# Weighted sums of the prompt attention in two bursts of 32 matmuls instead of one of 64

## The chip, the cores and the metric

The kernel runs on one core of one Trainium2 chip. The metric is the device time of one execution in microseconds (us). In the profile PE is TensorE's matmul row, PEld its weight loads, DVE is VectorE, ACT is ScalarE, POOL is GpSimd and SP is SyncE, whose queue (SPq) issues most DMAs. TensorE's clock has two levels here, 2.4 GHz (granted clock 1.0) and 1.2 GHz (0.5).

## What is computed

One step of a one-layer decoder trunk: an input projection to nine groups of columns, four token mixers side by side, an output projection, and a squared-ReLU MLP. There are 2048 prompt tokens and 8 x 4 sample tokens. What the change touches is the third mixer on the prompt, a strictly causal stick-breaking attention with four heads of 64 channels; its last line is the weighted sum of the values:

```python
def sb_block(q, k, v, q_start, sb_bias):
    z = jnp.einsum('bqhd,bkhd->bhqk', q, k) * (HEAD_DIM ** -0.5) + sb_bias[None, :, None, None]
    mask = kpos[None, :] < qpos[:, None]
    l = jnp.where(mask, jax.nn.log_sigmoid(-z), 0.0)
    later = jnp.flip(jnp.cumsum(jnp.flip(l, -1), -1), -1) - l
    w = jnp.where(mask, jnp.exp(jax.nn.log_sigmoid(z) + later), 0.0)
    return jnp.einsum('bhqk,bkhd->bqhd', w, v)
```

## The kernel before

**Dense work.** The projections and the MLP run over five blocks of 416 tokens. After the input projection the program is a list of steps. One step is one [128 x 1024] weight tile against one block: for each of eight groups of 128 channels it issues three matmuls of 128 x 416 (high part of the weights times high and low part of the activations, low part of the weights times the high part), 24 in all, into one of three PSUM banks. `dense(n)` writes one step; its loop over `groups` is the list of the eight. ACT and DVE split each weight tile into its two parts two steps ahead, read the finished bank, and prepare the next activations.

**Attention.** It is cut into 40 sets of (512 queries, a head, 512 keys), and each set into four units of 128 queries. The units are laid over time slots `tau`. The first 20 slots lie in the last steps of the input projection (two slots in a step). Those from 20 on lie one in a dense step, by the table `SLOT_AT`, in the first three of the MLP's stretches; this is the second part of the attention. In a slot TensorE computes the scores of one unit (lines 931 and 932), ACT takes two sigmoids of them, DVE makes the running product (`scan`), the product of both and its transpose in blocks of 32, in the following slots.

**Weighted sums.** `weigh(v)` takes all four units of set v at once: the keys are cut into 16 blocks of 32, and for every block there are four quarters of 32 rows, so that the array works as eight tiles of 32 x 64. The loop over `k` takes two blocks at a time, with 2 x 4 matmuls (line 946), in all 64. The trace shows each of them as two, so 128 matmuls and 128 weight loads. In the diagonal sets (queries and keys of one chunk) only the columns behind the diagonal are computed, 128, 96, 64 and 32 of them. The sums of all sets of a head and chunk pile up in PSUM banks 3 to 6. In front of the loop TensorE waits for the values (`s_vin3`), for the four transposes (`s_wt`) and, for the first set of a head, for the banks (`s_yc`); behind it, it signals `s_av`.

**Who waits for that signal.** After the last set of a head ACT copies half of the sums (`low_part`, line 1379) and DVE adds them; SP loads the next set's values (`load_v`, line 697); DVE's transposes of the set after next use the buffer anew. `weigh` is called in every fourth slot by `attention(tau)`, which stands ahead of `dense(n)` in the list of steps: scores, then weighted sum, then 24 matmuls of the step.

The order on each engine is the order in which the program writes it; nothing rearranges it. Instructions of TensorE come by DMA, on the queue that the profile calls q8.

Of the kernel before, what the change touches and what calls it, by code (L numbers as in the profile page):

```python
# [52 lines left out]
CHW = 512  # L53
# [56 lines left out]
def base_of(b):  # L110

    return PRE + STEPS_B * b
# [40 lines left out]
N_SETS, N_UNITS = len(SETS), 4 * len(SETS)  # L153
FIRST = [SETS.index((c, h, c)) for c in range(CH) for h in range(NH)]
FINAL = [SETS.index((c, h, 0)) for c in range(CH) for h in range(NH)]
ALONE = 20
SLOTS = N_UNITS + 4
SHARE = (46, 52, SLOTS - ALONE - 98)
SLOT_AT = {}
# [85 lines left out]
def build(nc, x_all, w_all, pvec, lnp, rows2, gates_a, gates_x, poolw, sbh, sbr, masks, ident_d, ck, cv, ptab,  # L245
          st_h, st_a, st_b, st_p, y_out, kv_out, so_out):
    ctx = ExitStack()
    with ctx:
# [10 lines left out]
        def sem(name):  # L259
            return ctx.enter_context(nc.semaphore(name))  # L260
# [63 lines left out]
        def x_hi(b):  # L324

            return xearly[:, b, 0, :, :] if b < 2 else xlate[:, b - 2, 0, :, :]

        def x_lo(b):

            return xearly[:, b, 1, :, :] if b < 2 else xlate[:, b - 2, 1, :, :]  # L330
# [146 lines left out]
        s_wt, s_av = sem("w_turned"), sem("av_done")  # L477
# [364 lines left out]
        def _(pe):  # L842
# [77 lines left out]
            def scores(t):  # L920

                v, i, w, top = unit(t)
                if i == 0:
                    pe.wait_ge(s_klo, v + 1)
                    if v in FIRST:
                        pe.wait_ge(s_qlo, FIRST.index(v) + 1)
                if t:
                    pe.wait_ge(s_sn, t)
                c, h, a = SETS[v]
                q = qs[:, (c * NH + h) % 2, i * P:(i + 1) * P]  # L930
                pe.matmul(PS[:, 7, 0:w], q, khl[:, v % 2, 0, 0:w], start=True, stop=False)  # L931
                pe.matmul(PS[:, 7, 0:w], q, khl[:, v % 2, 1, 0:w], start=False, stop=True).then_inc(s_z, 1)  # L932

            def weigh(v):

                c, h, a = SETS[v]
                pe.wait_ge(s_vin3, 64 * (v + 1))
                pe.wait_ge(s_wt, 4 * v + 4)
                if v in FIRST and v:
                    pe.wait_ge(s_yc, FIRST.index(v))  # L940
                for k in range(0, CHW // 32, 2):
                    first = k // 4 if a == c else 0
                    for quarter in range(4):
                        rows = slice(32 * quarter, 32 * quarter + 32)
                        for side in range(2):
                            ins = pe.matmul(PS[HD * side:HD * side + HD, 3 + quarter, first * 32:P], vq[rows, k + side, :],  # L946
                                            wt[rows, v % 2, first:4, k + side, :], start=(a == c and k == 0),
                                            stop=(a == 0 and k == CHW // 32 - 2))
                ins.then_inc(s_av, 1)

            def attention(tau):

                if tau < N_UNITS:
                    scores(tau)
                if tau % 4 == 2 and 0 <= (tau - 6) // 4 < N_SETS:
                    weigh((tau - 6) // 4)

            def attention_paused(done):

# [7 lines left out]
            def sample_new():  # L967

                pe.wait_ge(s_kqs, 96)
                for hp in range(2):  # L970
                    ins = pe.transpose(PS[0:SMP, 4, hp * P:(hp + 1) * P], kqs[:, 4 + hp, :], ident[:, :])
                ins.then_inc(s_vnt, 1)
                pe.wait_ge(s_qw, 2 * NH)
                pe.wait_ge(s_kn, 1)
                pe.wait_ge(s_yc, CH * NH)
                for half in range(2):
                    for b in range(4 * half, 4 * half + 4):
                        for hp in range(2):
                            for part in range(2):
                                ins = pe.matmul(PS[:, 3, half * SMP:(half + 1) * SMP], q_window(b, hp), knw[:, part, hp, :],  # L980
                                                start=(b % 4 == 0 and hp == 0 and part == 0), stop=(b % 4 == 3 and hp == 1 and part == 1))
                ins.then_inc(s_zd, 1)

            def sample_turn(u):

                pe.wait_ge(s_pg[u % RING], 64 * (u // RING + 1))
                if u < 2:
                    pe.wait_ge(s_vnw, 1)
                else:
                    pe.wait_ge(s_glo, u - 1)  # L990
                for hp in range(2):
                    for g in range(4):
                        ins = pe.transpose(PS[:, 4 + 2 * (u % 2) + hp, g * P:(g + 1) * P],  # L993
                                           pg[:, u % RING, g * 2 * P + hp * P:g * 2 * P + (hp + 1) * P], ident[:, :])
                ins.then_inc(s_ktr, 1)

            def sample_scores(u):

                b, q = u % DECB, u // 4
                pe.wait_ge(s_glo, u + 1)  # L1000
                if u % 4 == 0:
                    pe.wait_ge(s_zadd, q + 2)
                for hp in range(2):
                    for part in range(2):
                        ins = pe.matmul(PS[:, 3, :], q_window(b, hp), ghl[:, u % 2, part, hp * CHW:(hp + 1) * CHW],  # L1005
                                        start=(u % 4 == 0 and hp == 0 and part == 0), stop=(u % 4 == 3 and hp == 1 and part == 1))
                ins.then_inc(s_used, 1)
# [41 lines left out]
            def sample(r, half):  # L1049

                if r == K_AT - 1 and half == 0:
                    sample_new()
                u = 2 * (r - K_AT) + half
                first_of_window = u % 4 == 2
                if 0 <= u < 32 and first_of_window:
                    sample_turn(u)
                if 0 <= u - 2 < 32:
                    sample_scores(u - 2)
                if 0 <= u < 32 and not first_of_window:
                    sample_turn(u)  # L1060
                if half == 0 and 0 <= r - (K_AT + 19) < 4:
                    sample_w_turn(r - (K_AT + 19))
                m = 2 * (r - V_AT) + half
                if 0 <= m < 32:
                    sample_values(m)
                if half == 1 and r - V_AT in (9, 17):
                    sample_pairs((r - V_AT - 9) // 8)
# [13 lines left out]
            def dense(n, groups=range(KT)):  # L1081

                kind, b, q, i = step_at(n)
                if 0 in groups:
                    pe.wait_ge(s_wl, n + (NC_IN + 1))
                    if n >= 3:
                        free_bank(n - 3)
                    else:
                        pe.wait_ge(s_ev1, N_P - 2 + n)
                order = KORD if kind == "out" or (kind == "up" and q == 3 and i == KT - 1) else range(KT)  # L1090
                mh_, ml_ = (hh, hl) if kind == "down" else (ah, al)
                if kind == "late":
                    mh_, ml_ = x_hi(NB - 1), x_lo(NB - 1)
                out = PS[:, (N_P + n) % 3, 0:BLK]
                for g in groups:
                    k = order[g]
                    if b == 3 and n >= base_of(3) and g == 4:
                        sample(n - base_of(3), 1)
                    if n == KT and g == 2:
                        pe.wait_ge(s_oev, KT)  # L1100
                        second_half(xr, 0)
                    if n == KT + 1 and g == 4:
                        norm1_back(range(4))
                    if n in STAT_AT and g == 2:
                        norm1_stat(*STAT_AT[n])
                    if i == 0:
                        if kind == "down":
                            pe.wait_ge(s_hl, b * FT + q * KT + k + 1)
                        elif kind == "up" and q == 0:
                            pe.wait_ge(s_xl, (NB + b) * KT + k + 1)  # L1110
                        elif kind == "out" and g % 2 == 0:
                            pe.wait_ge(s_yl, b * 4 + g // 2 + 1)
                    w_h, w_l = w_at(w_hi(n), k), w_at(w_lo(n), k)
                    pe.matmul(out, w_h, mh_[:, k, :], start=(g == 0), stop=False)  # L1114
                    pe.matmul(out, w_h, ml_[:, k, :], start=False, stop=False)  # L1115
                    ins = pe.matmul(out, w_l, mh_[:, k, :], start=False, stop=(g == KT - 1))  # L1116
                    if kind == "up" and q == 3 and i == KT - 1 and b < NB - 1 and g in (1, 3, 5):
                        ins.then_inc(s_afree, 1)
                if KT - 1 in groups:
                    ins.then_inc(s_step, 1)  # L1120
# [1426 lines left out]
```

## Time and profile before

| | us |
|---|---|
| runs of the kernel before | 2401.73, 2406.59, 2409.28 |
| their median | 2406.59 |
| the profiled execution | 2408.72 |
| its span in the trace | 2407.1 |
| TensorE busy in the span | 2358.9 (98%) |
| VectorE busy | 1543.2 (64%) |
| ScalarE busy | 1180.2 (49%) |
| TensorE's mean granted clock | 0.995 |

The span is the time from the first to the last recorded instruction; 1.6 us of the execution lie around it. Rows of the timeline give the start, the duration, engine, line and operation, and in brackets how long the engine was idle before it and what ended that. Matmuls overlap: one of 416 columns takes 0.35 us, and the next starts 0.19 us after it, so that starts tell the pace. A row that merges several instructions gives the time from the first start to the last end.

### The profile page before, as it was taken

How to read it: one execution, taken by the hardware profiler on the slowest of the kernel's cores; microseconds unless marked ns; L12 is line 12 of the kernel's file. 1: busy time of each engine (PE TensorE's matmuls, PEld its weight loads, DVE VectorE, ACT ScalarE, POOL GpSimd, SP SyncE). 2: the span in 40 equal slices, each digit the busy share in tenths (PEclk: the TensorE clock that was granted, in tenths of full speed). 3: DMA queues.
4: the chain of work that ended last, by engine and by line, in shares of the span. 5: the costliest groups of instructions: out<-in, count | busy, mean ns of one | idle time of the engine just before them, and what ended most of it. 6: DMA issues, size and time to landing. Idle time of an engine off the chain costs nothing.

```text
span 2407.1 us, 44890 instructions
## 1 busy us (share of the span) xinstructions
PE 2358.9 (98%) x17487; PEld 2266.5 (94%) x17487; DVE 1543.2 (64%) x2195; ACT 1180.2 (49%) x1782; POOL 247.6 (10%) x528
## 2 busy tenths in 40 slices
PE   6999999999999999999999999999999999999998
PEld 6999999899999999999999999999999879999997
DVE  7545662656777678777788877768655435763435
ACT  5466522445645545556555465454455325444432
POOL 0012230200101000111110111100122130000000
PEclk9999999999999999999999999999999999999999
DMA  8434454644655434465453454443566674343332
GB/s 260 144 111 148 154 179 133 183 128 133 171 141 173 125 122 141 142 175 156 132 148 117 151 167 131 144 130 109 186 189 184 222 240 138 113 141 119 112 119 81
DMA packets 159222, 360.56 MB, mean 150 GB/s; under 512 B 39314, under 2 KB 82835, under 8 KB 158883
## 3 DMA queue, kind: packets, MB, share of 16 engines
q1 hardware_dynamic: 146658, 321.28, 44.0%
q0 software_dynamic: 12352, 36.42, 4.8%
q8 instruction: 139, 2.28, 0.4%
q14 instruction: 73, 0.59, 0.1%
HBM read 310.59 MB, written 47.02 MB: 149 GB/s over the span
## 4 chain that ended last, share of the span: by engine, by line
PE 94%; DVE 2%; ACT 2%; issue 1%; DMA 0%; SPq 0%; DVEq 0%; ACTq 0%
PE PS L1114 22%; PE PS L1116 22%; PE PS L1115 22%; PE PS L871 5%; PE PS L873 5%; PE PS L872 5%; PE PS L946 3%; PE PS L932 1%; PE PS L931 1%; PE PS L1005 1%; PE PS L993 1%; PE PS L1033 1%; PE PS L911 1%; PE PS L1147 1%; PE PS L851 1%
## 5 line engine op out<-in xcount | busy, mean ns | idle before, releaser
L1399 ACT ACTIVATE w_hi_lo<-w_raw 128x1024 fp32r<-128x1024 f32 x240 | 252.7, 1053 | 327.8 <-PE PS L1116 322.0
L1114 PE MATMUL PS<-a_hi,w_hi_lo 128*128 128x416 f32 x1080 | 383.5, 355 | 2.8 <-issue 1.4
L1116 PE MATMUL PS<-a_hi,w_hi_lo 128*128 128x416 f32 x1080 | 378.9, 351 | 1.3 <-issue 1.3
L1115 PE MATMUL PS<-a_lo,w_hi_lo 128*128 128x416 f32 x1080 | 378.1, 350 | 0.0
L1950 DVE TENSOR_TENSOR w_hi_lo<-w_raw,w_hi_lo 128x1024 fp32r<-128x1024 f32 x240 | 292.5, 1219 | 67.0 <-ACT w_hi_lo L1399 65.1
L1114 PE MATMUL PS<-h_hi,w_hi_lo 128*128 128x416 f32 x824 | 293.2, 356 | 0.0
L1116 PE MATMUL PS<-h_hi,w_hi_lo 128*128 128x416 f32 x824 | 290.1, 352 | 0.1
L1115 PE MATMUL PS<-h_lo,w_hi_lo 128*128 128x416 f32 x824 | 289.2, 351 | 0.0
L1977 DVE TENSOR_TENSOR h_lo<-h_full,h_hi 128x416 fp32r<-128x416 f32 x160 | 94.4, 590 | 247.0 <-ACT h_hi L1414 247.0
L1114 PEld LDWEIGHTS PS<-a_hi,w_hi_lo 128*128 128x128 f32 x1080 | 202.7, 188 | 12.5 <-issue 8.1
L1399 ACT ACTIVATE w_hi_lo_c<-w_raw 128x1024 fp32r<-128x1024 f32 x120 | 126.4, 1053 | 165.5 <-PE PS L1116 160.4
L1115 PEld LDWEIGHTS PS<-a_lo,w_hi_lo 128*128 128x128 f32 x1080 | 203.1, 188 | 4.7 <-issue 1.6
L1410 ACT ACTIVATE h_full<-PS 128x416 f32<-128x416 f32 x160 | 82.4, 515 | 250.6 <-PE PS L1116 244.4
L1116 PEld LDWEIGHTS PS<-a_hi,w_hi_lo 128*128 128x128 f32 x1080 | 202.4, 187 | 2.1
L1114 PE MATMUL PS<-a_hi,w_hi_lo_c 128*128 128x416 f32 x520 | 185.3, 356 | 1.9 <-DVE a_lo L1983 1.8
L1116 PE MATMUL PS<-a_hi,w_hi_lo_c 128*128 128x416 f32 x520 | 184.0, 354 | 0.0
L1115 PE MATMUL PS<-a_lo,w_hi_lo_c 128*128 128x416 f32 x520 | 183.2, 352 | 0.0
L1905 DVE TENSOR_TENSOR_SCAN n_prompt<-n_prompt 128x512 f32<-128x512 f32 (+3 forms) x160 | 177.3, 1108 | 4.2 <-POOL n_prompt L2451 3.5
L1950 DVE TENSOR_TENSOR w_hi_lo_c<-w_raw,w_hi_lo_c 128x1024 fp32r<-128x1024 f32 x120 | 146.4, 1220 | 36.3 <-ACT w_hi_lo_c L1399 35.1
L1114 PEld LDWEIGHTS PS<-h_hi,w_hi_lo 128*128 128x128 f32 x824 | 155.3, 189 | 8.3 <-issue 5.4
L1115 PEld LDWEIGHTS PS<-h_lo,w_hi_lo 128*128 128x128 f32 x824 | 155.6, 189 | 3.4
L1116 PEld LDWEIGHTS PS<-h_hi,w_hi_lo 128*128 128x128 f32 x824 | 155.0, 188 | 1.5
(322 smaller groups left out, 4814.7 us busy)
## 6 DMA issues: line engine op xcount, KB each, us to landing
w_raw<-w_all SPq DMA_DIRECT2D x380, 512.0 KB, 3.6
v_quarters<-v_scratch SPq DMA_DIRECT2D x160, 128.0 KB, 4.4
proj_scratch<-stage SPq DMA_DIRECT2D x70, 208.0 KB, 2.0
k_rows<-kv_out SPq DMA_DIRECT2D x80, 128.0 KB, 4.5
x_scratch<-x_full SPq DMA_DIRECT2D x20, 416.0 KB, 2.7
x_residual<-x_scratch SPq DMA_DIRECT2D x5, 1664.0 KB, 8.7
pages<-ck SPq DMA_DIRECT2D x64, 128.0 KB, 2.1
pages<-ck POOLq DMA_DIRECT2D x64, 128.0 KB, 2.5
```

The lines of the kernel that those rows point to most:

```text
L871: pe.matmul(out, w_h, x_hi(b)[:, k, :], start=(k == 0), stop=False)
L872: pe.matmul(out, w_h, x_lo(b)[:, k, :], start=False, stop=False)
L873: ins = pe.matmul(out, w_l, x_hi(b)[:, k, :], start=False, stop=(k == KT - 1))
L946: ins = pe.matmul(PS[HD * side:HD * side + HD, 3 + quarter, first * 32:P], vq[rows, k + side, :], wt[rows, v % 2, first:4, k + side, :], s ...
L1114: pe.matmul(out, w_h, mh_[:, k, :], start=(g == 0), stop=False)
L1115: pe.matmul(out, w_h, ml_[:, k, :], start=False, stop=False)
L1116: ins = pe.matmul(out, w_l, mh_[:, k, :], start=False, stop=(g == KT - 1))
L1399: act.activation(halves(w_hi(n)), raw_halves(n), ACT.Copy).then_inc(s_wh, 1)
L1410: act.activation(hf[:, f % 2, :], PS[:, (N_P + n) % 3, 0:BLK], ACT.Relu).then_inc(s_r, 1)
L1905: dve.tensor_tensor_scan(rev(n_t[:, 0:w]), rev(n_t[:, 0:w]), rev(n_t[:, 0:w]), n_t[:, w:w + 1], ALU.mult, ALU.bypass).then_inc(s_scan2, 1)
L1950: dve.tensor_tensor(halves(w_lo(n)), raw_halves(n), halves(w_hi(n)).bitcast(F32), ALU.subtract).then_inc(s_wl, 1)
L1977: dve.tensor_tensor(hl[:, i, :], hf[:, f % 2, :], hh[:, i, :].bitcast(F32), ALU.subtract).then_inc(s_hl, 1)
```

## The change

`weigh` gets a second argument, the list of the blocks that it takes. For the slots under 20 it is called as before, with all of them. From slot 20 on it is called twice in the same step: with the first eight blocks (32 matmuls) where it stood, and with the last eight in `dense(n)`, ahead of group 4, which is after 12 of the step's 24 matmuls. The signal comes behind the second call. The three waits in front of the loop are written in both calls. Of 40 sets the last 36 are split; 12 of these are diagonal sets.

```diff
-            def weigh(v):
+            def weigh(v, blocks):
...
                 if v in FIRST and v:
                     pe.wait_ge(s_yc, FIRST.index(v))
-                for k in range(0, CHW // 32, 2):
+                for k in blocks:
...
-                ins.then_inc(s_av, 1)
+                if blocks[-1] == CHW // 32 - 2:
+                    ins.then_inc(s_av, 1)
...
                 if tau % 4 == 2 and 0 <= (tau - 6) // 4 < N_SETS:
-                    weigh((tau - 6) // 4)
+                    weigh((tau - 6) // 4, range(0, CHW // 32, 2) if tau < ALONE else range(0, CHW // 64, 2))
...
                     k = order[g]
                     if b == 3 and n >= base_of(3) and g == 4:
                         sample(n - base_of(3), 1)
+                    if g == 4 and n in SLOT_AT and SLOT_AT[n] % 4 == 2 and (SLOT_AT[n] - 6) // 4 < N_SETS:
+                        weigh((SLOT_AT[n] - 6) // 4, range(CHW // 64, CHW // 32, 2))
```

TensorE's rows at a diagonal set of the second part before the change (`k_hi_lo` and `q_hi_lo` are the split keys and queries, `w_turned` the transposed weights, `v_quarters` the values, `h_hi` and `h_lo` the hidden activations, `w_hi_lo` the split weight tile, PS the PSUM banks):

```order
L931 MATMUL PS<-k_hi_lo,q_hi_lo 128x512 [waits sn_made]
L932 MATMUL PS<-k_hi_lo,q_hi_lo 128x512
L946 MATMUL PS<-w_turned,v_quarters 64x128 [waits y_head_made,w_turned,v_tile_in]
L946 MATMUL PS<-w_turned,v_quarters 64x128 x15
L946 MATMUL PS<-w_turned,v_quarters 64x96 x16
L946 MATMUL PS<-w_turned,v_quarters 64x64 x16
L946 MATMUL PS<-w_turned,v_quarters 64x32 x16
L1114 MATMUL PS<-h_hi,w_hi_lo 128x416 [waits relu_made,w_lo_made]
L1115 MATMUL PS<-h_lo,w_hi_lo 128x416
L1116 MATMUL PS<-h_hi,w_hi_lo 128x416
```

All 64 small matmuls stand between the scores and the step. The same place on TensorE in the changed kernel, where the step's lines are 1117 to 1119:

```order
L931 MATMUL PS<-k_hi_lo,q_hi_lo 128x512 [waits sn_made]
L932 MATMUL PS<-k_hi_lo,q_hi_lo 128x512
L946 MATMUL PS<-w_turned,v_quarters 64x128 [waits y_head_made,w_turned,v_tile_in]
L946 MATMUL PS<-w_turned,v_quarters 64x128 x15
L946 MATMUL PS<-w_turned,v_quarters 64x96 x16
L1117 MATMUL PS<-h_hi,w_hi_lo 128x416 [waits relu_made,w_lo_made]
L1118 MATMUL PS<-h_lo,w_hi_lo 128x416
L1119 MATMUL PS<-h_hi,w_hi_lo 128x416
```

The narrower half of the set has left the head of the step. It stands behind the step's first twelve matmuls, of which the last three are shown, with the three waits again:

```order
L1117 MATMUL PS<-h_hi,w_hi_lo 128x416
L1118 MATMUL PS<-h_lo,w_hi_lo 128x416
L1119 MATMUL PS<-h_hi,w_hi_lo 128x416
L946 MATMUL PS<-w_turned,v_quarters 64x64 [waits y_head_made,w_turned,v_tile_in]
L946 MATMUL PS<-w_turned,v_quarters 64x64 x15
L946 MATMUL PS<-w_turned,v_quarters 64x32 x16
L1117 MATMUL PS<-h_hi,w_hi_lo 128x416
L1118 MATMUL PS<-h_lo,w_hi_lo 128x416
```

In the other 24 split sets both halves are 32 matmuls of 64 x 128. No other engine's order changes.

## Rows read from the trace of the kernel before

**Rows 1.** Page, part 1: engine, busy us (share of the span), instructions.

```profile
PE 2358.9 (98%) x17487; PEld 2266.5 (94%) x17487; DVE 1543.2 (64%) x2195; ACT 1180.2 (49%) x1782; POOL 247.6 (10%) x528
```

**Rows 2.** Page, part 4: the chain that ended last, by engine.

```profile
PE 94%; DVE 2%; ACT 2%; issue 1%; DMA 0%; SPq 0%; DVEq 0%; ACTq 0%
```

**Rows 3.** Waits of PE: line, releaser, us in total, times, longest.

```profile
PE PS L946 <- issue: 8.1, 3, 4.6
PE PS L1114 <- issue: 3.5, 2, 2.1
PE PS L1116 <- issue: 1.3, 1, 1.3
```

**Rows 4.** Page, part 3: instruction queue of PE, packets, MB, share.

```profile
q8 instruction: 139, 2.28, 0.4%
```

**Rows 5.** Timeline of PE at a weighted sum of 128 columns throughout.

```profile
600.63 0.33 PE L932 MATMUL PS<-k_hi_lo,q_hi_lo 128*128 128x384 f32 x1
600.89 2.09 PE L946 MATMUL PS<-w_turned,v_quarters 32*64 32x128 f32 x128
602.92 0.45 PE L1114 MATMUL PS<-h_hi,w_hi_lo_c 128*128 128x416 f32 x1
603.21 0.35 PE L1115 MATMUL PS<-h_lo,w_hi_lo_c 128*128 128x416 f32 x1
603.39 0.35 PE L1116 MATMUL PS<-h_hi,w_hi_lo_c 128*128 128x416 f32 x1
```

**Rows 6.** Timeline of PE at a diagonal set.

```profile
623.10 1.80 PE L946 MATMUL PS<-w_turned,v_quarters 32*64 32x128 f32 x128
624.84 0.46 PE L1114 MATMUL PS<-a_hi,w_hi_lo 128*128 128x416 f32 x1
```

**Rows 7.** Line 946 alone in stretches of bursts: stretch, length, PE busy (x), PEld busy (x), clock.

```profile
600.88:601.82 0.94, 0.93 (x64) 0.93 (x68) 1.00 1.10 298
...
602.73:602.91 0.18, 0.18 (x19) 0.01 (x1) 1.00 0.20 21
```

**Rows 8.** Timeline of PE at four bursts, with the idle time in brackets.

```profile
666.70 1.80 PE L946 MATMUL PS<-w_turned,v_quarters 32*64 32x128 f32 x128
670.61 0.43 PE L1114 MATMUL PS<-h_hi,w_hi_lo_c 128*128 128x416 f32 x1 [2.11 <-issue]
...
799.87 2.07 PE L946 MATMUL PS<-w_turned,v_quarters 32*64 32x128 f32 x126 [0.28 <-DVE w_turned L1920]
805.12 0.43 PE L946 MATMUL PS<-w_turned,v_quarters 32*64 32x128 f32 x2 [3.17 <-issue]
805.47 0.46 PE L1114 MATMUL PS<-a_hi,w_hi_lo_c 128*128 128x416 f32 x1
...
1103.94 2.08 PE L946 MATMUL PS<-w_turned,v_quarters 32*64 32x128 f32 x128
1106.44 0.35 PE L1116 MATMUL PS<-a_hi,w_hi_lo 128*128 128x416 f32 x1
1108.18 0.34 PE L1114 MATMUL PS<-a_hi,w_hi_lo 128*128 128x416 f32 x1 [1.40 <-issue]
...
1490.83 0.35 PE L1116 MATMUL PS<-a_hi,w_hi_lo 128*128 128x416 f32 x1 [1.27 <-issue]
```

**Rows 9.** DMA queues in 666.6 to 668.0, then in 668.0 to 669.5.

```profile
q1 hardware_dynamic: 211, 0.49, 89.2%
...
q8 instruction: 1, 0.02, 3.7%
```

**Rows 10.** Stretches: length, busy of PE, PEld, DVE, ACT, POOL, then clock, DMA.

```profile
469.50:474.70 5.20, 5.20 (x20) 4.84 (x20) 0.68 (x1) 0.59 (x1) 0.00 (x0) 0.50 0.50 151
805.85:809.25 3.40, 3.40 (x12) 3.23 (x11) 0.00 (x0) 0.33 (x1) 0.00 (x0) 0.50 0.11 42
```

**Rows 11.** Timeline of ACT behind a last set of a head.

```profile
805.58 0.59 ACT L1379 ACTIVATE y_low_part<-PS 64x512 f32<-64x512 f32 x1 [2.09 <-PE PS L946]
811.88 0.52 ACT L1410 ACTIVATE h_full<-PS 128x416 f32<-128x416 f32 x1 [5.71 <-PE PS L1116]
```

## The prediction

> **What bounds the kernel now.** I read the page first: TensorE is busy for 98% of the span [rows 1], and the chain that ended last lies on it for 94% [rows 2]. So the time is the sum of what TensorE issues and of what makes it stop, and everything else counts only where TensorE waits for it. The waits of TensorE are the second view. In the weighted sums and in the step behind them the longest are put down to "issue": 8.1 us in three pieces at line 946, 3.5 us in two at line 1114 and 1.3 us at line 1116 [rows 3]. "Issue" is time in which no semaphore holds the engine, so I looked in the timeline for where they lie. Four lie in the second part of the attention, all inside a burst of weighted sums or a few matmuls behind it: 2.11, 3.17, 1.40 and 1.27 us [rows 8].
>
> What they wait for is the next piece of the program. The instruction queue moved 139 packets of together 2.28 MB [rows 4]; with 17487 matmuls and as many weight loads [rows 1] that is 252 of these for a packet, and with the separate waits about 256. In dense work two instructions take 0.19 us (the starts in [rows 5]), so a packet lasts about 24 us. A burst is 128 matmuls and 128 weight loads and uses up a whole packet in 2.0 us (600.89 to 602.92 in [rows 5]). If a packet begins just ahead of a burst, the next must come within 2 us. In the stall behind the burst of 666.70, the DMA queues show no instruction packet from 666.6 to 668.0, while data takes 89% of the engines; it moves only after 668.0 [rows 9], and TensorE goes on at 670.61. I read the mechanism so: the fetch of one packet starts when the one before begins to run, queues behind the data, and takes 3.9 us (666.70 to 670.61), 4.2 (1103.94 to 1108.18) or 5.3 (799.87 to 805.12) from the start of the burst [rows 8].
>
> The Trainium skill (Runtime: NRT & Kernel Launch, Instruction fetch mechanics) says the sequencer fetches the next block of 256 instructions while it executes the current one, and that crossing a block is mostly hidden. The size agrees with the 252 of the rows; that it is hidden does not hold at these four bursts.
>
> **What the change takes away.** With the split, a packet that begins at the first half covers 128 instructions in 0.94 us [rows 7], the end of that burst (0.2 us), 24 instructions of the step in 12 x 0.19 = 2.3 us, and some 104 of the second half in 0.8 us: about 4.4 us with the entry in place of 2.0. Against the needs of 3.9, 4.2 and 5.3 us two stalls vanish and one keeps 0.9 us; of the fourth, 1.27 us behind a burst, I count all as gone. The stalls cost, beyond the normal pace: 666.70 to 670.61 is 3.9 us against 1.74 us for an equal diagonal set [rows 6], so 2.2; 3.17 us plus some 0.2 for the restart, 3.4; and 1.40 and 1.27 us, each with 0.16 us more (a matmul lasts 0.35 and the pace is 0.19), 1.6 and 1.4. Together 8.6 us, less the 0.9 left: 7.7. The 36 further wait instructions shift where packets begin, so other bursts will be hit than now, but for any of them the floor is near 4.4 us.
>
> **The clock.** After the idle 3.17 us the granted clock is 0.50 in 805.85 to 809.25, 12 matmuls in 3.4 us [rows 10]; at half speed that loses 1.7 us. With that stall cut to about 1 us I count these 1.7 us as gained; it is the stretch whose cause the change touches, and at worst they stay. The stretch 469.5 to 474.7 at 0.50 [rows 10] stands behind a stall in the first part, which is not split; it stays. Gain: 7.7 + 1.7 = 9.4 us.
>
> **What the change adds.** A second burst means entering and leaving the small tiles once more. Entering: the start of line 932 to the first small matmul is 0.26 us, where its pace with 384 columns is 0.18 (a little under the 0.19 for 416), so 0.1. Leaving: the last small matmul stands 0.18 us before the dense one [rows 7], which in a burst would be followed after 0.014 (2.03 / 128, counted with its end), so 0.17; then the first dense matmul takes 0.29 us to the second, where the pace is 0.19 [rows 5], so 0.1. Together 0.37 us, and with the extra wait instruction 0.38. The halves themselves gain nothing: the first 64 small matmuls take 0.94 us of the 2.03, the rest 0.91 and the end 0.18. For 24 sets I take 0.39. For the 12 diagonal ones the narrow half may run a little faster after the step's twelve matmuls, since it is then not behind 64 others; I take 0.32. Sum: 9.4 + 3.8 = 13.2 us. No row shows a burst in the middle of a step. Bounds: from 36 x 0.25 = 9 us (entry and one end alone) to 36 x 0.45 = 16 us; I stay near the rows of whole bursts, which are the same operations.
>
> The Trainium skill (TensorEngine Tiling (Array Packing), Key Properties) says that a change of the tiling mode drains TensorE. It gives no price; the 0.1 + 0.17 + 0.1 us of the rows agree with it, and it speaks against the change, which makes 36 such pairs more.
>
> **Edits that I count at nothing.** The signal comes 2.7 us later in the step. ACT's copy (0.59 us, 12 times in this part) then starts about 4.8 us into a step of 7 us and ends at 5.4; ACT's next work for TensorE waits for the end of that step anyway (idle 5.71 us in [rows 11]). If that cover were gone it would cost 12 x 0.6 = 7 us. The next values are loaded by SP in the following slot, behind the signal in either case, and are used four slots later. DVE's transposes need the signal of two sets before. The step's first twelve matmuls begin about 1 us earlier against the preceding step; their weight tile was split two steps before. The waits in the second call are already met. So the accumulation in the step's bank only pauses.
>
> **Sum.** 2408.7 + 13.2 - 9.4 = 2412.5 us by the profiled execution. That one is 2.1 us above the median of 2406.6. What differs between runs is probably such stalls, part of which the change removes; so I take off half of it, 1.0: **2411.5 us**.
>
> **The rivals.**
> A, the forecast, 2411.5, on its own from 2406 to 2417 by the bounds of the switch (9 to 16 us) and by gains of 7 to 10. Chance 0.60.
> B, slower: the stalls stay. The fetch needs over 4.4 us at most bursts hit, because data holds the DMA engines longer than the split adds, or because the idle is no fetch at all. For it speaks the 5.3 us at 799.87 and the 89% of [rows 9]; against it the 3.9 and 4.2. It decides where the fetch takes over 6 us: then only 1 to 2 us are gained, and 2408.7 + 13.2 - 2 = 2420. Chance 0.20. By the skill's rule that the crossing is hidden, nothing would be there to gain, 2408.7 + 13.2 = 2422; the four stalls speak against it, and it is part of B.
> C, a cheaper switch: in the middle of a step TensorE's queue is full, and only the entry of 0.1 us counts: 36 x 0.12 = 4 us, 2408.7 + 4 - 9.4 = 2403. For it: nothing waits there on a semaphore. Against it: the 0.29 us behind the burst is there in both. Chance 0.15.
> D, the split costs nothing, since each half runs at the pace of a full queue: 2408.7 - 9.4 = 2399. Chance 0.05.
>
> **How the numbers follow.** A measurement of this kernel can tell about 0.3%, 7.2 us, from no change: under 2399.4 or over 2413.8. A gives 0.47 within and 0.13 above, B 0.20 above, C 0.15 within, D 0.05 below. Faster 0.05, same 0.62, slower 0.33. The range leaves out D and the far end of B: 2403 to 2420.
>
> **What would show it.** Right: two merged rows of line 946 in a step, with a first dense matmul behind each that takes about 0.3 us to the next, and a step with both about 0.4 us longer in sum than before; no "issue" over 1.5 us at lines 946 or 1117 to 1119 after 570 us; no stretch at clock 0.50 between 480 and 1600 us; the stall in the first part as it was. Wrong: stalls of 2 us and more in or behind a second half (B); a second burst that lengthens the step by 0.2 us or less (C, D); or ACT's copy followed by a wait of TensorE on ACT.

## The result: 0.2% slower, 2411.1 us

| | before | after |
|---|---|---|
| median of 20 runs each, us | 2406.11 | 2411.11 |
| lowest and highest, us | 2400.11, 2409.28 | 2403.97, 2413.24 |
| ratio, 95% interval | | 1.0023, 1.0016 to 1.003 |
| profiled execution, us | 2408.72 | 2413.07 |
| its span, us | 2407.1 | 2411.5 |
| mean granted clock | 0.995 | 0.996 |
| second part of the attention in the trace, us | 1022.4 | 1026.6 |

The forecast was 2411.5. The difference of 5.0 us is surely there, but under the 0.3% that was called no change.

The second part of the attention is measured between two stops of TensorE that stand in every kernel of this document: the scores that wait for ACT ahead of set 4, and the dense matmul that waits for DVE's `a_lo` behind set 39. In the timeline of before and then of after they read (start, duration, engine, line, idle time before and what ended it):

```profile
573.93 0.50 PE L931 MATMUL PS<-k_hi_lo,q_hi_lo 128*128 128x512 f32 x1 [0.42 <-ACT n_prompt L1372]
...
1596.33 0.43 PE L1114 MATMUL PS<-a_hi,w_hi_lo_c 128*128 128x416 f32 x1 [0.61 <-DVE a_lo L1983]
```

```profile
574.37 0.50 PE L931 MATMUL PS<-k_hi_lo,q_hi_lo 128*128 128x512 f32 x1 [0.43 <-ACT n_prompt L1375]
...
1600.98 0.43 PE L1117 MATMUL PS<-a_hi,w_hi_lo_c 128*128 128x416 f32 x1 [0.61 <-DVE a_lo L1986]
```

1596.33 - 573.93 is 1022.4 us, 1600.98 - 574.37 is 1026.6. So 4.2 of the 4.4 us by which the spans differ lie where the change was made. Differences of a few us are read on this measure below, because the ends of the program add their own scatter.

### The profile page after: what moved, and what is told of

Read it like the earlier page. It is cut to its first block, busy times and chain, and to the rows that moved or that the text cites. A ratio compares the mean times of both kernels' runs of the same rounds, so it can differ in the third digit from the quotient of the medians.

```text
span 2411.5 us, 44926 instructions
## 1 busy us (share of the span) xinstructions
PE 2373.2 (98%) x17487; PEld 2266.5 (94%) x17487; DVE 1544.1 (64%) x2195; ACT 1182.1 (49%) x1782; POOL 246.5 (10%) x528
## 3 DMA queue, kind: packets, MB, share of 16 engines
q8 instruction: 139, 2.28, 0.4%
## 4 chain that ended last, share of the span: by engine, by line
PE 95%; DVE 2%; ACT 1%; issue 1%; DMA 0%; SPq 0%; DVEq 0%; ACTq 0%
PE PS L1117 23%; PE PS L1119 22%; PE PS L1118 22%; PE PS L871 5%; PE PS L873 5%; PE PS L872 5%; PE PS L946 4%; PE PS L932 1%; PE PS L931 1%; PE PS L1006 1%; PE PS L994 1%; PE PS L1034 1%; PE PS L911 1%; PE PS L1150 1%; PE PS L851 0%
## 5 line engine op out<-in xcount | busy, mean ns | idle before, releaser
L1117 PEld LDWEIGHTS PS<-a_hi,w_hi_lo 128*128 128x128 f32 x1080 | 202.7, 188 | 12.7 <-issue 8.2
L1117 PEld LDWEIGHTS PS<-h_hi,w_hi_lo 128*128 128x128 f32 x824 | 155.3, 188 | 9.9 <-issue 6.6
L1973 DVE TENSOR_TENSOR mlp_sum<-mlp_sum,PS 128x416 f32<-128x416 f32 x117 | 68.7, 587 | 139.4 <-PE PS L1119 138.0
```

## The profile after

Part 1 of the page, engines, and the waits of TensorE in the whole span:

```profile
PE 2373.2 (98%) x17487; PEld 2266.5 (94%) x17487; DVE 1544.1 (64%) x2195; ACT 1182.1 (49%) x1782; POOL 246.5 (10%) x528
```

```profile
PE PS L946 <- issue: 4.6, 2, 4.2
PE PS L1117 <- DVE a_lo L1986: 1.8, 3, 0.6
PE PS L1117 <- DVE w_hi_lo L1953: 1.3, 1, 1.3
```

TensorE does the same 17487 matmuls as in [rows 1] and is busy for 14 us more, of which the span shows only 4.4: it stands still less. Of the "issue" in [rows 3] (8.1, 3.5 and 1.3 us) 4.6 are left, and 4.2 of them are the stall at 465 us in the first part, which is not split. All four stalls of [rows 8] are gone. The set of the longest, 3.17 us, now reads:

```profile
802.19 1.20 PE L946 MATMUL PS<-w_turned,v_quarters 32*64 32x128 f32 x64 [0.28 <-DVE w_turned L1923]
...
805.79 1.21 PE L946 MATMUL PS<-w_turned,v_quarters 32*64 32x128 f32 x64
```

The half clock behind it went too. In stretches of after (length, busy of PE, granted clock, DMA share) only the one behind the stall of the first part stands, as in [rows 10], and then none for 1241 us:

```profile
469.10:475.90 6.80, 6.47 (x23) 0.50 0.57 158
...
480.00:1721.00 1241.00, 1236.35 (x10706) 1.00 0.49 141
```

What the split costs is read from the starts around the two bursts of a step. A set of 128 columns throughout:

```profile
601.44 0.33 PE L932 MATMUL PS<-k_hi_lo,q_hi_lo 128*128 128x384 f32 x1
601.70 1.21 PE L946 MATMUL PS<-w_turned,v_quarters 32*64 32x128 f32 x64
602.84 0.46 PE L1117 MATMUL PS<-h_hi,w_hi_lo_c 128*128 128x416 f32 x1
603.14 0.35 PE L1118 MATMUL PS<-h_lo,w_hi_lo_c 128*128 128x416 f32 x1
...
605.02 0.35 PE L1119 MATMUL PS<-h_hi,w_hi_lo_c 128*128 128x416 f32 x1
605.30 1.21 PE L946 MATMUL PS<-w_turned,v_quarters 32*64 32x128 f32 x64
606.44 0.46 PE L1117 MATMUL PS<-h_hi,w_hi_lo_c 128*128 128x416 f32 x1
606.74 0.35 PE L1118 MATMUL PS<-h_lo,w_hi_lo_c 128*128 128x416 f32 x1
```

From the matmul ahead of a burst to the second one behind it are 1.70 and 1.72 us, together 3.42. The whole burst of [rows 5] takes 2.58 (600.63 to 603.21). The second burst stands among dense matmuls, whose two paces of 0.19 would be there without it: 3.42 - 0.38 - 2.58 = 0.46 us a set. The same places at a diagonal set:

```profile
579.69 0.40 PE L932 MATMUL PS<-k_hi_lo,q_hi_lo 128*128 128x512 f32 x1
...
581.40 0.35 PE L1118 MATMUL PS<-h_lo,w_hi_lo 128*128 128x416 f32 x1
...
583.28 0.35 PE L1119 MATMUL PS<-h_hi,w_hi_lo 128*128 128x416 f32 x1
...
584.67 0.35 PE L1118 MATMUL PS<-h_lo,w_hi_lo 128*128 128x416 f32 x1
```

These are 1.71 + 1.39 = 3.10 us. A whole diagonal burst without a stall, from the kernel of the first experiment below:

```profile
578.04 0.40 PE L952 MATMUL PS<-k_hi_lo,q_hi_lo 128*128 128x512 f32 x1
578.37 1.80 PE L974 MATMUL PS<-w_turned,v_quarters 32*64 32x128 f32 x128
580.10 0.46 PE L1147 MATMUL PS<-h_hi,w_hi_lo 128*128 128x416 f32 x1
580.40 0.35 PE L1149 MATMUL PS<-h_lo,w_hi_lo 128*128 128x416 f32 x1
```

It takes 2.36, and 3.10 - 0.38 - 2.36 = 0.36 us a set. Over all, 24 x 0.46 + 12 x 0.36 = 15.4 us.

ACT's copy behind the last set of a head comes later in the step, as forecast, and still ends ahead of what TensorE waits for; ACT is idle for 1.86 us behind it where [rows 11] had 5.71:

```profile
807.03 0.60 ACT L1382 ACTIVATE y_low_part<-PS 64x512 f32<-64x512 f32 x1 [1.21 <-PE PS L946]
809.48 0.52 ACT L1413 ACTIVATE h_full<-PS 128x416 f32<-128x416 f32 x1 [1.86 <-PE PS L1119]
```

## Where the packets begin

The forecast took it that a stall needs a packet of the program that begins "just ahead of a burst". The trace allows this to be counted. Counted in the order of the program, a packet holds 256 instructions. Every stall of before (the four of [rows 8] and the one of 4.6 us in the first part) stands at the same place of such a block: with the instructions of TensorE in the trace numbered from 0, the matmul behind the stall has a number that is 193 to 195 more than a multiple of 256. And it starts 2.4 or 2.5 us behind the transfer of an instruction packet, all five times. A matmul with its weight load is two instructions for the dense ones and four for the small ones, and what stands in the program as two waits in a row is one. Four steps with one set are 470, so a packet's begin moves on by 42 from one burst to the next (2 x 256 - 470), and about one burst in six is hit. In before a packet begins within 16 instructions of the start of seven bursts out of 40: set 3 (11 ahead), 8 (at the start), 14 (4 ahead), 16 (12 behind), 22 (8 behind), 29 (16 behind), 35 (12 behind). Sets 3, 8, 14, 22 and 35 are the long stalls; 16 loses 0.2 us (two dense matmuls start at 975.03 and 975.45, 0.42 apart where the pace is 0.19), and 29 none that shows; no other burst of before loses any. In after, with the repeated waits, packets still begin within 16 instructions of the first half of five split sets: 8 (4 ahead), 14 (14 ahead), 16 (at the start), 22 (10 ahead) and 29 (9 ahead). None of them makes TensorE stop, so the split does cover the fetch; the waits have not merely moved it away.

This gives a lever that does not touch the bursts: met waits (on a semaphore that has had its value since the start) written in among the dense matmuls push the packets on. All experiments but e5 and e11 use it:

```diff
+            def pad(count):
+
+                for _ in range(2 * count):
+                    pe.wait_ge(s_const, 32)
...
                     pe.matmul(out, w_h, mh_[:, k, :], start=(g == 0), stop=False)
+                    pad(PAD_AT.get((n, g), 0))
                     pe.matmul(out, w_h, ml_[:, k, :], start=False, stop=False)
```

`PAD_AT` spreads the pairs of waits over the steps between two bursts, at most a few in a group. The kernels ran in three sessions, each on one chip with the kernel before beside them:

| kernel | bursts from set 4 | a packet begins | median, us | its session's before | second part, us |
|---|---|---|---|---|---|
| e1 | whole | 128 into each | 2396.88 | 2404.49 | 1011.9 |
| e2 | whole | at each start | 2470.25 | 2404.49 | 1091.7 |
| e3 | halves | 128 from each start | 2410.51 | 2404.49 | 1027.0 |
| e4 | halves | at each start | 2415.6 | 2404.49 | 1029.4 |
| e5 | six sets in halves | as before | 2399.64 | 2402.24 | 1015.4 |
| e6 | whole | 128 into each, and into set 3 | 2393.11 | 2402.24 | 1011.8 |
| e7 | quarters | 128 from each start | 2432.11 | 2402.24 | 1046.9 |
| e8 | whole | 17 or more from any start | 2394.97 | 2402.24 | 1012.6 |
| e9 | whole | as e1, sets 0 to 3 free too | 2391.28 | 2406.43 | 1012.2 |
| e10 | whole | 17 or more from any start | 2393.45 | 2406.43 | 1013.5 |
| e11 | halves, the changed kernel | as after | 2410.65 | 2406.43 | 1026.6 |

## Experiment 1 and 2: the same whole bursts, packets in their middle and at their start

The two differ in nothing but how many met waits stand between the bursts: 1857 pairs put a packet's begin 128 instructions into each burst from set 4 on, 1729 put it at the start.

> The kernel before, with whole bursts, and with already met waits put between matmuls of the dense steps of the second attention part (1857 of them in all, 42 for most sets), so that in each of the 36 bursts from set 4 on a new packet of 256 instructions begins exactly in the middle of the burst, 128 instructions in. Theory F (the idle time at the bursts is the fetch of the next packet, and it comes where a packet begins within some 16 instructions of the burst's start): no issue idle over 0.3 us in or behind a burst after 570 us, no half clock between 480 and 1600 us, and some 2396 us (2411.1 of the changed kernel less 15.0 for 36 splits), up to 2400 if the added waits cost 2 ns each. Rival N (the idle time belongs to these places for another reason, data traffic or semaphores, and the split only moved it): stalls stay at the sets where they were, 2406 us or more.

> As e1, but the packets begin exactly at the first instruction of each of the 36 bursts (1729 added waits), so that every burst is one packet. Theory F: nearly every burst is followed by a stall of 1.5 to 3.5 us, in sum 50 to 90 us, with stretches at half clock behind the longest of them; 2450 to 2495 us. Rival N: the same time as e1, within 3 us, since only the place of met waits differs.

Measured: 2396.88 us (2391.13 to 2398.26, ratio to before 0.9964, 0.9948 to 0.998) and 2470.25 us (2465.47 to 2475.04, ratio 1.027, 1.0236 to 1.0303). All 36 bursts of the second are followed by a stop, with 0.39 to 3.39 us of idle time; of the first none. In e2's timeline the burst of 647.59:

```profile
647.59 2.09 PE L974 MATMUL PS<-w_turned,v_quarters 32*64 32x128 f32 x128
653.07 0.43 PE L1147 MATMUL PS<-a_hi,w_hi_lo 128*128 128x416 f32 x1 [3.39 <-issue]
```

DMA queues of e2 (packets, MB, share) in 647.5 to 650.6, then in 650.6 to 651.6:

```profile
q1 hardware_dynamic: 522, 1.13, 93.4%
```

```profile
q8 instruction: 1, 0.02, 6.0%
```

For three microseconds behind the start of the packet no instruction packet moves, while data fills the queues; it moves behind 650.6, and TensorE goes on 2.4 us later. That the burst uses up the packet before the next one is there is thereby shown. The other end of the scale is the burst of 1087.94. Its packet moves at 1088.09, 0.14 us behind the start of the burst, and the stop behind it is the shortest of all:

```profile
1090.43 0.43 PE L1147 MATMUL PS<-h_hi,w_hi_lo 128*128 128x416 f32 x1 [0.39 <-DVE w_hi_lo L1984]
```

Over the 36 bursts of e2 the packet moves between 0 and 3.1 us behind the start of the burst, and TensorE goes on 2.3 to 3.0 us behind it; so the length of a stop follows how late the packet moves. That the data is what holds it back is only seen beside it: no run changed the data.

Such stops bring the half clock with them. Two of the ten stretches of e2 in this part (length, busy of PE, clock, DMA share):

```profile
653.60:656.90 3.30, 3.30 (x11) 0.50 0.44 137
...
1042.70:1046.00 3.30, 3.30 (x11) 0.50 0.98 287
```

And the waits of TensorE in 560 to 1700 us:

```profile
PE PS L1147 <- DVE w_hi_lo L1984: 25.7, 17, 2.8
PE PS L1147 <- issue: 23.8, 10, 3.4
```

Here is a trap. DVE's weights were ready; the first instruction of the new packet also carries a wait for them, and the view seems to give the stop to the last semaphore that it knows. All 36 stops, whichever name they carry, stand at the same place of the block and 2.3 to 3.0 us behind an instruction packet. In e1, with the same DVE, neither line is there.

The difference of e2 and e1 is 73.4 us by the medians (e2 has two runs), 79.8 by the second part. The rows account for the latter: the 36 stops hold 63.0 us of idle time, and ten stretches at half clock cost some 1.7 us each.

## Experiment 3 and 4: the same two, with halves

They are e1 and e2 with sets 4 to 39 split as in the change, but without the repeated waits:

```diff
-                    weigh((tau - 6) // 4)
+                    v = (tau - 6) // 4
+                    weigh(v, range(0, 8 if v in SPLIT_SETS else CHW // 32, 2))
...
+                    if g in (4,) and SLOT_AT.get(n, 0) % 4 == 2 and (SLOT_AT[n] - 6) // 4 in SPLIT_SETS:
+                        at = 8 * (1 + (4,).index(g))
+                        weigh((SLOT_AT[n] - 6) // 4, range(at, at + 8, 2))
```

> As e1, with every set from 4 on split in two halves as in the changed kernel, but without the repeated waits in the second half. The packet begins at the end of the first half. Theory S (the change costs the switch between full matmuls and small tiles once more, 0.45 us in each of 24 sets and 0.36 us in each of 12 diagonal ones, 15.0 us): 15 us over e1, 2411 us, with no stall either. Rival A (the later signal costs time through ScalarE's copy or the SP queue, and the switch is cheaper): the two bursts of a step cost less than 0.3 us more than one, and TensorE waits for ScalarE or VectorE in the steps behind; the difference to e1 is spread over waits. Rival C (the switch costs nearly nothing when no packet begins near a burst): under 5 us over e1.

> As e2 (a packet begins at the first instruction of each first half), with every set from 4 on split. The packet then lasts 4.3 us in place of 1.8. Theory F: a stall is left only where the fetch takes more than that, at most a third of the 36, each 0.3 to 1.5 us; 2411 to 2425 us, so the split, which costs 15 us in e3, saves 40 us or more here. Rival N: the same as e3 within 3 us.

Measured: 2410.51 us (2406.31 to 2413.38, ratio 1.0025, 1.0015 to 1.0035) and 2415.6 us (2412.86 to 2417.94, ratio 1.0046, 1.0031 to 1.0062). With no stall to be had, the split costs 2410.51 - 2396.88 = 13.6 us by the medians. The two markers give it without the scatter of the ends; they stand in e1, then in e3:

```profile
572.73 0.50 PE L951 MATMUL PS<-k_hi_lo,q_hi_lo 128*128 128x512 f32 x1 [0.42 <-ACT n_prompt L1406]
...
1584.60 0.43 PE L1147 MATMUL PS<-a_hi,w_hi_lo_c 128*128 128x416 f32 x1 [0.61 <-DVE a_lo L2017]
```

```profile
573.13 0.50 PE L951 MATMUL PS<-k_hi_lo,q_hi_lo 128*128 128x512 f32 x1 [0.42 <-ACT n_prompt L1406]
...
1600.09 0.43 PE L1147 MATMUL PS<-a_hi,w_hi_lo_c 128*128 128x416 f32 x1 [0.60 <-DVE a_lo L2017]
```

1011.9 and 1027.0 us, so 15.1 us for 36 cuts. (The profiled run of e3 happens to lack the half clock at the sample stage that the others have, which brings its span closer.)

With the packets at the starts the halves give back what they cost and much more: e4 is 54.7 us under e2. The split leaves the fetch its time, as the forecast said, and in the profiled run it is enough at 34 of 36 bursts. One of the two where it is not is the one of 647.59 again, where e2 stood for 3.39 us:

```profile
647.58 1.08 PE L974 MATMUL PS<-w_turned,v_quarters 32*64 32x128 f32 x51
649.17 0.47 PE L974 MATMUL PS<-w_turned,v_quarters 32*64 32x128 f32 x13 [0.51 <-issue]
```

The other is at 1220.19, with 0.26 us. That first set starts at 643.97, so the packet lasted until 648.66, 4.7 us, where the forecast had 4.4. The profiled run of e4 is the fastest of its five, though (2412.86, the slowest 2417.94), and the median is 5.1 us above that of e3: by the medians, packets at every start still cost the split kernel some 5 us.

## Experiment 5: only the six sets that are hit

`SPLIT_SETS` holds 8, 14, 16, 22, 29 and 35, and no packet is moved.

> The kernel before with only six of its sets split in two halves (8, 14, 16, 22, 29, 35), those at whose start a packet begins (4 instructions ahead to 16 behind), without repeated waits, so that no packet moves. Theory F and S: all stalls of the second part go (8.6 us, and two smaller ones of together 0.6, and the half clock of 1.7 us), for 6 x 0.44 = 2.6 us; about 8 us under the kernel before of these runs, 2397 to 2398 us. Rival: the split of all sets was needed (stalls at unsplit sets appear in other runs): 2401 us or more.

Measured: 2399.64 us (2398.16 to 2402.02, ratio 0.9988, 0.9978 to 0.9997). The sign is right, the size is a third of what was expected. The profile shows why: its second part takes 1015.4 us, which is what was expected of it (1011.9, six cuts of 0.42 and one stop of 0.70 us idle at 802.53), and the 1022.4 of before's profiled run are more than a typical run has on this chip. By the medians before lies only 2.6 us above e5, whose second part is 3.5 above one without stalls, so a typical run of before loses here some 6 us in these stalls, not 10.5. On the other chips it is more: where before and a kernel that is split and has no stall left in its profile were run together, they lie 5.0, 6.0 (e3) and 4.2 us (e11) apart, which with a split of 15.1 us leaves 9 to 11 us for the stalls.

## Experiment 6: the stall of the first part too

As e1, with 117 of the pairs that stood ahead of set 4 put between sets 2 and 3 instead, which are two steps apart.

> e1 (no split, a packet begins in the middle of each burst) and the same for set 3 of the first part, with 117 added met waits between sets 2 and 3. Theory F: the stall of 3.7 to 4.8 us in set 3 goes too, and with it the stretch at half clock behind it (2.6 us): 6 to 7 us under e1, 2389 to 2391 us. Rival N: set 3 stalls since data holds all DMA engines from 462 to 467 us whatever the packet's place: the same as e1, 2396 to 2397 us.

Measured: 2393.11 us (2392.32 to 2393.47, ratio 0.996, 0.9946 to 0.9974), e1 less 3.8 where 6 to 7 were expected (across two chips). The stall of set 3 and its half clock are gone, as the window of e6 shows:

```profile
460.00:480.00 20.00, 19.69 (x216) 1.00 0.74 220
```

The rest went into the waits themselves. In e6's timeline behind set 2:

```profile
451.68 0.45 PE L891 MATMUL PS<-x_late,w_hi_lo 128*128 128x416 f32 x1
452.36 0.43 PE L895 MATMUL PS<-x_late,w_hi_lo 128*128 128x416 f32 x1 [0.23 <-issue]
...
454.39 0.35 PE L891 MATMUL PS<-x_late,w_hi_lo 128*128 128x416 f32 x1
454.89 0.43 PE L895 MATMUL PS<-x_late,w_hi_lo 128*128 128x416 f32 x1 [0.15 <-issue]
```

0.68 and 0.50 us stand between starts that are 0.19 apart elsewhere. The burst of set 3 starts 16.1 us behind that of set 2 (449.94 to 466.00), in e1 12.7: a met wait pair costs 3.4 / 117 = 0.03 us where many stand close together. Spread at one in two or three matmuls they cost nothing that can be seen: e8 has 1694 pairs fewer than e6, and its second part is no shorter (1012.6 against 1011.8 us). The split kernels say the same: e3 with 1857 pairs takes 1027.0 us, the changed kernel with none 1026.6.

## Experiment 7: quarters

e3 with four bursts of 16 matmuls in a step, ahead of groups 0, 2, 4 and 6.

> As e3, but with four bursts of 16 matmuls in a step (at its head and ahead of groups 2, 4 and 6). Theory S1 (each entry and exit costs the same 0.4 us): three further switches in place of one, 3 x 13.6 = 41 us over e1, 2437 us. Theory S2 (an entry and exit cost 0.09 + 0.18 + 0.11 us, but the first 32 small matmuls behind dense ones go at 13.4 ns each and those behind them at 16, because TensorE's queue is then empty): a quarter takes 0.21 + 0.4 us, four of them 2.4 us against 2.22 of a whole burst, so 5 to 8 us over e1, 2402 to 2405 us, less than the two halves of e3.

Measured: 2432.11 us (2430.21 to 2432.46, ratio 1.012, 1.0101 to 1.0139), and 1046.9 us for the second part, 35.0 above e1. One of the four bursts in e7's timeline:

```profile
600.82 0.69 PE L974 MATMUL PS<-w_turned,v_quarters 32*64 32x128 f32 x32
601.44 0.46 PE L1147 MATMUL PS<-h_hi,w_hi_lo_c 128*128 128x416 f32 x1
601.74 0.35 PE L1149 MATMUL PS<-h_lo,w_hi_lo_c 128*128 128x416 f32 x1
```

The rows explain the 35 us. From the start of the burst to the first dense matmul are 0.62 us, 0.30 more to the second; with the entry of 0.28 and less the two paces of 0.38 a quarter costs 0.82; the first, behind the scores, is entered in 0.27, so four cost 3.27. A whole burst costs 2.58 less two paces of 0.19, 2.20. That makes 1.07 x 24 = 25.7 us, and by the same rows of a diagonal set 0.81 x 12 = 9.7. The lower of the two expectations miscounted the matmuls of a quarter, and the higher one (2437) left out that the small matmuls of a burst do not come evenly: from the first start to the last, 32 take 0.42 us, 64 take 0.94, and 128 take 1.83. Two halves are then 0.05 us longer than the whole, four quarters 0.13 shorter. So a cut costs 0.42 us when a burst is halved, and 0.32 us for each of three when it is quartered. Most of it lies at the entry and at the exit (0.09, 0.19 and 0.11 us), which every cut has.

## Experiments 8 to 11: few waits, all stalls, and the changed kernel beside them

e8 takes just 163 pairs, so that no packet begins within 16 instructions of the start of a burst. e9 is e1 with 160 pairs spread over fifty steps of the input projection, where they are cheap, in place of the 117, and has 1857 in all, as many as e1 and e6. (The "1974" and "2000" of two expectations count some of them twice.) e10 does both with 221 pairs; its table is

```diff
+PADS = {0: 160, 4: 29, 15: 12, 28: 4, 39: 16}
```

(the set ahead of which they stand, and how many; 0 is the input projection). e11 is the changed kernel once more.

> As e6, with 163 added waits in place of 1974: 117 ahead of set 3, 30 ahead of set 4, 12 ahead of set 15 and 4 ahead of set 28. No packet then begins within 16 instructions of a burst's start; the nearest are 17 ahead and 17 behind. Theory F: 0 to 3 us over e6, with at most a short stall or two of under 1 us where a packet begins 17 to 25 instructions from a burst's start, less what 1800 waits cost, if they cost anything; 2388 to 2393 us. Rival N: as e1 or the kernel before, 2396 us or more.

> Whole bursts. As the kernel with 128 in every burst (a packet of the program begins 128 instructions into each whole burst from set 4 on, by met waits ahead of it), but with 160 pairs of met waits spread over steps 24 to 73 of the input projection instead of 117 in two steps ahead of set 3: packets then begin 177, 61, 201 and 85 instructions behind the start of the bursts of sets 0 to 3. Theory: the stall of set 3 (4.6 us) and its half clock (1.7 us) are gone as in the kernel that had the 117 ahead of set 3, and the 3.3 us that those cost in a cluster are gone too: 2393.1 less 3.3, about 2390. Rival: the waits cost the same however they are spread; then 2393.

> Whole bursts, and only some 220 pairs of met waits instead of 2000: 160 spread over the input projection, and 29, 12, 4 and 16 ahead of sets 4, 15, 28 and 39, so that no packet begins from 16 ahead to 16 behind the start of any burst. Theory (only packets that begin near the start of a burst make TensorE stop): no stall anywhere but at the sample stage, 2390 to 2392, as the kernel with 2000 pairs. Rival (the nearest ones, 17 and 21 behind a start, still stall in some executions): 2393 to 2395, with a wider scatter.

> The changed kernel as it stands, beside the kernels without stalls on the same chip. By the split's price of 13.6 to 15 us and the stall that it leaves in the first part: 2389.8 + 4.6 + 1.7 + 14.3, about 2411. Rival (it has stalls that its profile did not show): 2414 and more, with a scatter as wide as that of the kernel before.

Measured:

| | median, us | lowest, highest | ratio to before | 95% interval |
|---|---|---|---|---|
| e8 | 2394.97 | 2392.97, 2396.36 | 0.9965 | 0.9954 to 0.9975 |
| e9 | 2391.28 | 2390.79, 2392.82 | 0.9938 | 0.9923 to 0.9953 |
| e10 | 2393.45 | 2392.85, 2399.02 | 0.9953 | 0.994 to 0.9967 |
| e11 | 2410.65 | 2405.12, 2413.08 | 1.0019 | 1.0009 to 1.0028 |

e9 is the fastest kernel of this study, 15.2 us under before and 19.4 under the changed one on the same chip, with the computation and the order of all engines as before. Over e6 it gained 1.8 us, across two chips, where 3.3 were hoped for. TensorE, no longer held up, now meets a later wait of 1.5 us, for the activations of the next stage, which e6 does not have:

```profile
482.05 0.46 PE L1151 MATMUL PS<-a_hi,w_hi_lo_c 128*128 128x416 f32 x1 [1.50 <-DVE a_lo L2021]
```

e10 went as its rival said. Its nearest packets are too near in some runs: one that begins 25 behind the start of a burst ends twelve dense matmuls behind it, and there its profile shows a stop (and another of 0.33 us idle at 1206.00, where the packet begins 17 behind):

```profile
643.42 0.35 PE L1154 MATMUL PS<-a_hi,w_hi_lo 128*128 128x416 f32 x1
644.40 0.46 PE L1151 MATMUL PS<-a_hi,w_hi_lo 128*128 128x416 f32 x1 [0.64 <-issue]
```

So 16 instructions are no edge behind which nothing happens; the need of the fetch varies, and each instruction of distance is worth more where dense work stands between.

e11 came out as expected by the price of the split, and the same as in the first comparison.

The runs also tell where the scatter of before and after comes from. Kernels with the stall of set 3 mostly spread over 4 to 9 us (before, after, e1, e3, e5; e7, with 4 runs, over 2.3), those without it and with packets in the middle (e6, e9) over 1.2 and 2.0, in 5 and 4 runs. But e8 and e10, which are without it and have packets nearer to the bursts, spread over 3.4 and 6.2. So it is likely that stalls make the scatter, that of set 3 above all; the numbers of runs are small, and no run but the profiled ones shows its stalls.

## Why the prediction was right

**What bounds the kernel, and what the stalls are: right.** TensorE's issue sets the time; the stalls are fetches. Experiments 1 and 2 show it by moving the packets and nothing else, and the part of rival B by which the crossing of packets costs nothing falls with them: 73 us lie between the two.

**The gain: right in kind, sized a little low.** The forecast took 8.6 us of stalls, 0.9 left over, and 1.7 of clock: 9.4. The second part without any stall is 1011.9, in before's profiled run 1022.4: 10.5 us were there to gain, and after's profile shows all of them gone. The working (4.4 us of cover against needs of 3.9 to 5.3) is borne out by e4, where packets stand at every start: nearly all covered, two short stops left, and a cover of 4.7 us. The 1.7 us for the clock fit too: from 805.47 to 809.40 TensorE starts 12 dense matmuls in 3.93 us, which take 2.28 at its usual pace. The signs that the forecast named all came: two bursts with 0.30 us behind each, no "issue" over 1.5 us and no half clock in this part, and the stall of the first part as it was.

**The cost: the term that was mis-sized.** 24 x 0.39 + 12 x 0.32 = 13.2 us were predicted; after less e1 is 14.7, e3 less e1 15.1, the sum from single rows 15.4. The three fixed parts were right in kind. Missing were some 0.03 us in the exit (0.20 against 0.17; the working divides 2.03 by 128 and writes 0.014 for 0.016, which changes nothing) and 0.03 in the pace: the forecast read the second 64 of a whole burst, 0.91 us, as no faster than the first 64, 0.94, and neglected the difference, which each cut gives away. For the diagonal sets 0.36 against 0.32. The bounds of 9 and 16 us held.

**The sum and the median: right number, partly by luck.** 2408.7 + 14.9 - 10.5 = 2413.1, as the profiled run of after has it. (14.9 lies between 14.7 and 15.1. With 14.7, which is read from after itself, the sum comes out by construction; 15.1 is the independent price.) The 1.0 us for the median was taken off because the change was thought to remove part of what differs between runs. That reason failed: after scatters as much as before (9.3 us against 9.2), and its profiled run is 2.0 above its median too, though the second part has no stall left in it. Over its 20 runs the median of before is 2.6 us under its profiled run; why both profiled runs lie high is not shown. So the cost was 1.5 to 1.9 us too low, the gain 1.1 too low, and the median of after lies 2.0 and not 1.0 under its profiled run. Together they came out 0.4 us from the forecast, and that they cancel so well is luck.

**The rivals.** B (stalls stay) falls: after's profile has none in this part, and with packets at every start the split kernel stands for 0.51 and 0.26 us at two bursts of 36 in its profile, some 5 us by the medians (e4 less e3), where the whole bursts cost 73. C and D fall by the 0.46 and 0.36 us that a set costs. That ACT's copy would hold up TensorE did not happen; its margin shrank from 5.7 to 1.9 us.

**What the prediction did not see** is that the stalls depend on where packets fall by chance, and that this can be set for nothing. The change pays 15 us at 36 bursts to cure some 6 to 11 us at five of them (sets 8, 14, 16, 22 and 35); e5, which pays at six alone, is 2.6 us faster than before, and the kernels that pay at none are 7 to 15 us faster (in e6, e8, e9 and e10 the stall of the first part is gone too; in e1, with 7.6 us, it is not).

## What to carry to other kernels

A stop of TensorE put down to "issue" behind a dense run of small instructions can be a fetch of the program: count the instructions from one such stop to another, and if they are a multiple of the packet, move the packet and not the work. A change between small and large tiles and back cost some 0.4 us each time here, so it is to be bought where a stall stands and not everywhere. And where the thing to be cured differs between executions, one profiled execution may show it at its worst.

## What the hardware showed that was not expected

- Moving the begin of program packets by half a burst, with waits that are always met, changes the time of the kernel by 73.4 us in 2400 (e2 against e1). The Trainium skill (Runtime: NRT & Kernel Launch, Instruction fetch mechanics) calls the crossing mostly hidden; in dense work that agrees with the trace (before has 139 packets, and of its stops at a packet's end each lies in a burst or within 12 instructions behind one), in bursts it does not.
- From the transfer of an instruction packet to TensorE's next matmul it takes 2.4 us (650.6 to 653.07 in e2; 2.3 to 3.0 over its 36 stops), and the transfer begins 0 to 3.1 us behind the first instruction of the packet before.
- A pair of met waits costs 0.03 us when some sixty stand in a step, and nothing that is seen when they are a fifth as dense.
- In a burst of 128 columns the starts of the first 40 small matmuls come in eights, 0.007 us apart, with 0.06 us between one eight and the next (0.11 behind the first); behind them most come every 0.007 or 0.017 us. It is so in before, e1 and after alike; nothing here shows why.
